# A transformer on one core: the order of the first stage's work and of the end of the sparse stages

## The reference, cut to what matters

```python
def swiglu(x, w_gate, w_up, w_down):
    return (jax.nn.silu(x @ w_gate) * (x @ w_up)) @ w_down

# first block, per layer l (stage 0 is the first line for l = 0)
y = swiglu(rms_norm(x, ffn1_pre_g[l]), ffn1_w_gate[l], ffn1_w_up[l], ffn1_w_down[l])
x = x + 0.5 * rms_norm(y, ffn1_post_g[l])
# second block, per layer l ("sparse" stage, then "relu" stage)
u_pool, q, k, v, iq, ik, iw = jnp.split(rms_norm(x, g_pre_mix[l]) @ w_in[l], ...)
mix = jnp.concatenate([pool_mixer(u_pool, ...), dsa_attention(q, k, v, iq, ik, iw, topk)], -1) @ w_out[l]
x = x + rms_norm(mix, g_post_mix[l])
f = jnp.square(jax.nn.relu(rms_norm(x, g_pre_ffn[l]) @ w_ff1[l])) @ w_ff2[l]
x = x + rms_norm(f, g_post_ffn[l])
```

## Time and profile before

| what | us |
|---|---|
| median of 3 runs | 1866.11 (1865.77 to 1866.67) |
| the profiled execution | 1865.99 |
| its span in the trace | 1864.0 |
| PE busy | 1839.5 (99%) |
| DVE busy | 1315.5 (71%) |
| ACT busy | 1042.3 (56%) |
| POOL busy | 216.2 (12%) |
| moved from memory | 336.62 MB, 181 GB/s over the span |

### The profile page before, as it was taken

One profiled execution on the slowest core, in us unless ns is written; L12 is line 12 of the kernel. 1 busy time (PEld: TensorE's weight loads), 2 busy tenths in 40 slices (PEclk: granted clock), 3 DMA queues, 4 the chain that ended last, 5 costly groups with the idle time before them and its releaser, 6 DMA issues.

```text
span 1864.0 us, 27880 instructions
## 1 busy us (share of the span) xinstructions
PE 1839.5 (99%) x10911; PEld 1610.8 (86%) x10911; DVE 1315.5 (71%) x1734; ACT 1042.3 (56%) x1503; POOL 216.2 (12%) x264
## 2 busy tenths in 40 slices
PE   6999999999999999999999999999999999999998
PEld 6888899888888888889998988888888888888887
DVE  5766758776766776676687677666886667787665
ACT  5555545655655565555466566556755545665453
POOL 1010101010100011001021000002201111301110
PEclk9999999999999999999999999999999999999999
DMA  8585663355566557766344446655546654636561
GB/s 296 182 295 189 171 199 119 114 181 170 185 201 202 181 185 234 256 170 224 124 136 139 168 138 224 202 179 168 180 136 205 196 186 165 226 100 206 181 200 71
DMA packets 229971, 339.46 MB, mean 182 GB/s; under 512 B 22278, under 2 KB 178064, under 8 KB 229840
## 3 DMA queue, kind: packets, MB, share of 16 engines
q1 hardware_dynamic: 221968, 307.91, 50.2%
q0 software_dynamic: 7872, 29.78, 4.8%
HBM read 336.62 MB, written 1.05 MB: 181 GB/s over the span
## 4 chain that ended last, share of the span: by engine, by line
PE 93%; DVE 5%; ACT 1%; DMA 1%; issue 0%; DVEq 0%; SPq 0%; ACTq 0%
PE ps L1670 90%; PE ps L1675 3%; DVE wlo L1095 2%; DMA raw<-ffn_w_gate 1%; DVE region L1103 1%; DVE mlo L1095 1%; DVE xn L1095 0%; DVE ahl L1095 0%; ACT region L690 0%; DVE xs L1103 0%; DVE region L1593 0%; DVE sm L1591 0%; DVE hlo L1095 0%; DVE small L1111 0%; ACT ahl L690 0%
## 5 line engine op out<-in xcount | busy, mean ns | idle before, releaser
L1095 DVE TENSOR_TENSOR wlo<-raw,whi 128x1024 fp32r<-128x1024 f32 (+2 forms) x458 | 560.2, 1223 | 174.1 <-ACT whi L690 138.4
L690 ACT ACTIVATE whi<-raw 128x1024 fp32r<-128x1024 f32 (+2 forms) x458 | 482.5, 1054 | 66.2 <-PE ps L1670 16.0
L1670 PE MATMUL ps<-ahl,whi 128*128 128x512 f32 (+1 forms) x1920 | 433.5, 353 | 0.3
L1670 PEld LDWEIGHTS ps<-ahl,whi 128*128 128x128 f32 x1920 | 331.4, 190 | 43.0 <-DVE hlo L1095 0.9
L690 ACT ACTIVATE region<-ps 128x512 f32<-128x512 f32 (+2 forms) x260 | 150.1, 577 | 336.0 <-PE ps L1670 251.7
L1670 PE MATMUL ps<-whi,ahl 128*128 128x512 f32 (+2 forms) x1120 | 303.1, 348 | 8.7 <-DVE ahl L1095 7.7
L1670 PE MATMUL ps<-ahl,wlo 128*128 128x256 f32 x1568 | 269.3, 283 | 0.0
L1670 PEld LDWEIGHTS ps<-ahl,wlo 128*128 128x128 f32 x1568 | 233.4, 191 | 11.9
L1670 PEld LDWEIGHTS ps<-whi,ahl 128*128 128x128 f32 x1120 | 197.4, 190 | 35.0 <-DVE ahl L1095 10.0
L1095 DVE TENSOR_TENSOR mlo<-raw,mhi 128x1024 fp32r<-128x1024 f32 x130 | 160.8, 1237 | 47.2 <-ACT mhi L690 37.7
L1670 PE MATMUL ps<-wlo,ahl 128*128 128x512 f32 (+2 forms) x560 | 191.3, 342 | 0.0
(11 more groups left out here) (166 smaller groups left out, 2380.1 us busy)
## 6 DMA issues: line engine op xcount, KB each, us to landing
raw<-w_ff SPq DMA_DIRECT2D x64, 1024.0 KB, 5.4
raw<-ffn_w_gate SPq DMA_DIRECT2D x44, 1024.0 KB, 5.3
raw<-ffn_w_up SPq DMA_DIRECT2D x44, 1024.0 KB, 5.5
raw<-ffn_w_down SPq DMA_DIRECT2D x44, 1024.0 KB, 4.9
raw<-w_in SPq DMA_DIRECT2D x38, 1024.0 KB, 6.1
raw<-w_out SPq DMA_DIRECT2D x16, 1024.0 KB, 4.9
raw<-xa_wk SPq DMA_DIRECT2D x8, 1024.0 KB, 5.2
raw<-xa_wv SPq DMA_DIRECT2D x8, 1024.0 KB, 5.0
```

Of the source, the lines that this page charges most:

```text
L690: e.activation(o, i, f, **kw).then_inc(*act.did(*names))
L1095: e.tensor_tensor(o, a, b, op).then_inc(*dve.did(*names))
L1670: m = e.matmul(o, l, r, start=start, stop=stop)
```

## The change

It has two parts that act. The first is a function `begin` on ACT, DVE and PE in place of the `turn` of stage 0. SP loads the first gain itself, right behind the tokens m = 0; item 0 comes as two transfers of half an item with a semaphore each; POOL sends the second gain when item 0 has landed. PE turns the identity 6 times ahead of the first tokens and 12 times behind them, into a bank that nobody reads, and may start with the first four of eight row blocks when the first half of item 0 is split (`lo_half`). The product's order is now item 0 for both tiles, then item 1 for both. DVE weighs the first half of tokens m = 1 before the second half of item 0 is split; ACT sums the squares of tile 0 before it takes the tokens (1, 0). The second part is in the sparse stages: DVE's `head(2)` stands behind `out(0)` and `out(1)`, and the item of `take(s, "w_out2", 2)` is split earlier, on DVE in two pieces around `out(2)` and `turned(3)`, on ACT ahead of `turned(3)`. In `turn` the branches for stage 0 go away; other stages keep their order.

```diff
             x_half(0)
+            e.dma_start(GV[:, 0:DM], gains[0][1][0][1].partition_broadcast(128)).then_inc(*gain0_in.did(("gain", 0)))
             e.dma_start(CS[:, 0:128], A["c_small"][:, 0:128]).then_inc(*const_in["ident"].did(("in",)))
-            load(0)
+            dst, src = raw_of(0).rearrange("p (k n) -> p k n", k=8), items[0][1]
+            e.dma_start(dst[:, 0:4, :], src[:, 0:4, :]).then_inc(*half_in.did(("raw", 0)))
+            e.dma_start(dst[:, 4:8, :], src[:, 4:8, :]).then_inc(*raw_in[0].did(("raw", 0)))
             x_half(1)
             load(1)
...
-            gain_load(0)
+            q.wait_ge(*raw_in[0].at("raw", 0))
             gain_load(1)
...
@@ in scalar @@
+            def begin():
+                i0, i1 = first_items(0)
+                split_to(i0, halves=1)
+                halves(0, 0, 0, 0)
+                split_to(i0)
+                halves(0, 0, 1, 1)
+                row_square(0, 0)
+                halves(0, 1, 0, 2)
+                split_to(i1, halves=1)
+                halves(0, 1, 1, 3)
+                split_to(i1)
+                row_square(0, 1)
+                split_to(i1 + 1)
+                scales(0)
@@ in scalar, sparse @@
                 exps("s", l, 3, 256, sP, 1.0)
+                take(s, "w_out2", 2)
                 turned(3)
                 post_square(s + 1, 0)
-                take(s, "w_out2", 2)
                 halves(s + 0.5, 1, 1, TILEBANK[1])
                 take(s, "w_out2", 3)
...
@@ in vector @@
+            def begin():
+                i0, i1 = first_items(0)
+                for h in range(2):
+                    q.wait_ge(*x_in[0].at("x", 0))
+                    weighted(0, 0, h)
+                split_to(i0, halves=1)
+                halves(0, 0, 0, 0)
+                q.wait_ge(*x_in[1].at("x", 1))
+                weighted(0, 1, 0)
+                split_to(i0)
+                halves(0, 0, 1, 1)
+                halves(0, 1, 0, 2)
+                weighted(0, 1, 1)
+                split_to(i1, halves=1)
+                halves(0, 1, 1, 3)
+                mean_square(0, 0)
+                split_to(i1)
+                mean_square(0, 1)
+                ts(eq, qm, TIMES[1] ** -2.0 * EPS, None, ALU.mult, ALU.bypass, ("eq", 0))
+                split_to(i1 + 1)
@@ in vector, sparse @@
                 select(1)
-                head(2)
                 out(0)
                 out(1)
+                head(2)
...
                 turned(2)
+                split_to(number[s, "w_out2", 2] + AHEAD, halves=1)
                 out(2)
                 turned(3)
+                take(s, "w_out2", 2)
                 weigh(s + 1, 0)
                 out(3)
                 renew(s + 1, 0, (0,))
                 halves(s + 0.5, 1, 1, TILEBANK[1])
                 renew(s + 1, 0, (1,))
-                take(s, "w_out2", 2)
                 take(s, "w_out2", 3)
...
@@ in tensor @@
+            def begin():
+                def awake(n):
+                    for _ in range(n):
+                        turned(PS[:, 6, 0:128], IDN, 128)
+                it = first_items(0)
+                awake(6)
+                turn_tokens(0, 0, 0)
+                turn_tokens(0, 0, 1)
+                awake(12)
+                for i, n in enumerate(it):
+                    hi, lo = halves_of(n)
+                    for m in range(2):
+                        ms = slice(m * 128, (m + 1) * 128)
+                        for k in range(8):
+                            if (i, m, k) == (0, 0, 4):
+                                turn_tokens(0, 1, 0)
+                            if (i, m, k) == (0, 1, 0):
+                                turn_tokens(0, 1, 1)
+                            if (i, m, k) == (1, 1, 7):
+                                turn_scales(0)
+                            q.wait_ge(*dve.at("lo_half" if k < 4 else "lo", n))
+                            q.wait_ge(*dve.at("a", 0, m, k // 4))
+                            ...
+                            three(PS[:, m, i * 256:(i + 1) * 256], ahv[:, k, ms], alv[:, k, ms], hi[:, k, :], lo[:, k, :], k == 0, k == 7, *names)
```

More of the change, by code:

```diff
@@ L300, in build @@
         w1_in = Done(sem("w1_in"), 16)
+        half_in, gain0_in = [Done(sem(n), 16) for n in ("half_in", "gain0_in")]
         stored = Done(sem("stored"), 16)
-        every = [pe, act, dve, pool, *raw_in, *gain_in, *x_in, *const_in.values(), region_in, mem_in, w1_in, stored]
+        every = [pe, act, dve, pool, *raw_in, *gain_in, *x_in, *const_in.values(), region_in, mem_in, w1_in, half_in, gain0_in, stored]
         IDN = CS[:, 0:128]
@@ L1125, in split_to @@
                     q.wait_ge(*act.at("hi", n, h))
-                    tt(lo[:, c], raw[:, c], hi[:, c].bitcast(F32), ALU.subtract, *([("lo", n)] if h else []))
+                    tt(lo[:, c], raw[:, c], hi[:, c].bitcast(F32), ALU.subtract, ("lo", n) if h else ("lo_half", n))
             def take(s, tag, c, ahead=AHEAD):
@@ L1132, in gain_here @@
                 i = gain_no[s, which]
-                q.wait_ge(*gain_in[i % NG].at("gain", i))
+                q.wait_ge(*(gain_in[i % NG] if i else gain0_in).at("gain", i))
                 return gain_of(s, which)
@@ L1655, in sparse @@
                 renew(s + 1, 0, (1,))
-                take(s, "w_out2", 2)
                 take(s, "w_out2", 3)
+            begin()
             for s in range(12):
-                turn(s)
+                if s:
+                    turn(s)
                 {"ffn": ffn, "relu": ffn, "hybrid": hybrid, "memory": memory, "sparse": sparse}[kind_of(s)](s)
@@ L1699, in turn_tokens, with turn_scales @@
                     blocks(s, m, half, 2 * m + half)
+            def turn_scales(s):
+                for m in range(2):
+                    q.wait_ge(*pool.at("r2", s, m))
+                    turned(PS[:, 7, m * 128:(m + 1) * 128], r2[:, m:m + 1].broadcast_to([128, 128]), 128, *([("r2_turned", s)] if m else []))
+            def begin():
[9 more added lines that the diff above has]
+                    hi, lo = halves_of(n)
+                    for m in range(2):
+                        ms = slice(m * 128, (m + 1) * 128)
[8 more added lines that the diff above has]
+                            q.wait_ge(*dve.at("a", 0, m, k // 4))
+                            names = [("used", n)] if (m, k) == (1, 7) else []
+                            names += [("first", 0, m)] if (i, k) == (1, 7) else []
+                            three(PS[:, m, i * 256:(i + 1) * 256], ahv[:, k, ms], alv[:, k, ms], hi[:, k, :], lo[:, k, :], k == 0, k == 7, *names)
             def turn(s):
                 it, by_k = first_items(s), BY_K[kind_of(s)]
-                def scales():
-                    for m in range(2):
-                        q.wait_ge(*pool.at("r2", s, m))
-                        turned(PS[:, 7, m * 128:(m + 1) * 128], r2[:, m:m + 1].broadcast_to([128, 128]), 128, *([("r2_turned", s)] if m else []))
                 parts = [(i, n, kk) for i, n in enumerate(it) for kk in range(items[n][2])]
@@ L1738, in turn @@
                 if kind_of(s) != "sparse":
-                    ahead[1][count - 1] = scales
+                    ahead[1][count - 1] = lambda: turn_scales(s)
                 ahead[0][count * 3 // 4 if by_k else 11] = lambda: turn_tokens(s, 1, 0)
```

46 lines of the change are left out of this document (15 added, 31 removed).

## The result

The changed kernel takes 1856.91 us (median of 6 runs, 1856.78 to 1857.21); the kernel before, in the same rounds, 1866.66 (1865.77 to 1866.79). The ratio is 0.9949, 95% interval 0.9936 to 0.9962: 9.75 us, 0.5%, faster. Forecast were 1859.3 us and a range whose ends the prediction works out as 1857.6 and 1862.8.

A forecast was written before the change was run, and what follows sets the result against it. PE, busy 99% of the span, was taken as the bound, so only its idle or slow time could be won: 1865.99 - 5.0 (begin) - 1.8 (sparse ends) = 1859.2, with 0.1 to the median 1859.3 us; range 1857.6 to 1862.8.

The forecast's parts named there:

- The begin: Stretch up to the turning of stage 0's scales: would end at 26.3 instead of 31.3 us, gain 5.0 us.
- curve + 1.9 us: Begin: each load lands 1.9 us after the summed GB/s curve of before passes the bytes queued up to it.
- Rival (e): Begin: item 0's split load brings nothing, first half landing no sooner than second; costs 0 to 0.5 us, counted within forecast's 0.58.
- The lower bound: Lower end, 1857.6 us: landings at the begin with 0.6 us of lag instead of 1.9 (-1.3), and head(2) (-0.4).
- The sparse ends: Ends of both sparse stages: PE's whole wait for DVE's low half goes, 0.9 us in each, 1.8 us in all.
- the head's 0.4: Sparse stages: head(2) behind the two outputs, at most 0.2 us a stage; nothing in the forecast, -0.4 at the lower end.
- (a): Begin: turnings don't bring the fast pace, or PE falls back in pauses; 1860.5 to 1861.6 us, chance 0.19.
- the full 1.2 us: Begin: first 12 matmuls and 4 turnings run slow, pushing ACT's tokens (1,0) and all behind them by 1.2 us.
- (b): Sparse ends: DVE's half split waits for a late ACT, exchanging one wait for another; 1860.2 to 1861.1 us, chance 0.09.
- (c): By 45 us: loads 5 and 6 meet POOL's queue, giving back 2 to 3 of 5.0 us; 1861.3 to 1862.3, chance 0.10.
- (d): Begin: a crawling gain transfer on SP's queue delays all loads behind it; slower, 1870.3 us if it takes 16 us, chance 0.04.
- the 1859.2 of the sum: Whole kernel: profiled 1865.99 less 5.0 for the begin and 1.8 for the sparse ends, before 0.1 to the median.

The follow-up runs named there:

- the second trace: The changed kernel run once more, unchanged, beside the kernel before: 1856.83 us, ratio 0.9946.

## Why the prediction was off

**What held.** That only PE's idle and low-paced time can be given back, and where it lies; that the first product would start near 12.2 (11.88, and 12.32 in the second trace); that it would run at 0.12 us a matmul; that a row of work on DVE would then set the end (DVE's order of these steps, changed in one point, moves the end by 0.8 us or more); that the shift would stay until the first sparse end; that nothing comes back behind the sparse ends; that the gain on SP's queue would cost nothing.

**The begin: 5.65 us instead of 5.0.** The step that failed is the landing, "curve + 1.9 us", and with it the sentence that DVE's row starts from x1's landing. The first half came at 8.6 instead of 9.1, the second at 10.1 instead of 10.7, x1 at 11.4 instead of 12.2. The curve of bytes was taken from a trace in which two queues work; with the gain on the same queue the lag behind the bytes is smaller. The changed kernel's own line of GB/s, summed in the same way, passes the 1.64 MB of the first half at 7.6 us and the 2.69 MB of x1 at 10.3, and they land 1.0 and 1.1 us later, not 1.9. With the gain on POOL's queue again x1 landed at 12.8, 2.3 us behind the same number of bytes: the lag goes with the second queue.
The forecast had x1 land at 12.2, just when DVE would have been done with the first half's work (12.2 too), so it couldn't tell which of the two sets the end, and it chose x1. The traces say the first half: in the changed kernel DVE was busy until 11.73 with x1 there since 11.4, and with item 0 in one transfer the scales moved by 1.5 to 1.9 us though x1 came only 0.4 later. Rival (e) put that price at 0 to 0.5, for the same wrong reason. Since the first half came 0.5 us sooner, DVE's row ran some 0.4 us ahead of the forecast throughout (weighing at 11.83 instead of 12.2, tokens (1,1) done at 18.3 instead of 18.75), and PE's last stretch took 7.3 us instead of 7.5: 25.66 with the scales' turning, 26.3 forecast. The lower bound had a smaller lag, with 1.3 us for it. 0.4 us of the 5.65 are luck: the traced run of the changed kernel had the earliest rise of the pace of all, and in the second trace the gain is 5.3.

**The sparse ends: 3.1 us instead of 1.8** (3.09 between the traces of before and after, 3.17 in the experiments). Two terms were wrong. First the size of the wait. I took the 0.91 us of idle time in brackets. That counts from the modelled end of the last matmul, 1390.66. But a matmul of 512 columns is followed by the next after 0.23 us: it would have started at 1390.49 and started at 1391.57, 1.08 us late. With a second small pause in the first matmuls behind it (1392.96 to 1393.29 where 0.24 is usual) and 0.08 us of a longer first matmul, 1.23 us were to be won at each end, 2.5 in all. Take the distance between starts, not the idle time. Second, head(2), which I put at nothing, with 0.4 us as the bound: it is 0.5. The reason was not the one weighed, PE getting the outputs sooner, but DVE's pause of 0.46 us in the middle of its pooled steps. That pause stood in the timeline of before, named as DVE waiting for itself:

```profile
1365.76 1.00 DVE L1103 SCALAR_TENSOR_TENSOR ahl<-ps,sm,ahl 128x256 fp32r<-128x256 f32 x2 [0.46 <-DVE ahl L1103]
```

My range put the head's 0.4 and the smaller lag together, but held the wait's size for known: that is why the time fell below it.

**The rivals.** (a) came true in part: the pace rises during the turnings or with the first matmuls, at 9.7 to 12.4 us in kernels with this begin, and a late rise costs 0.4 us through the turnings themselves, which then run too long. It isn't the full 1.2 us, because PE doesn't start the product at the low pace. The rule of the Trainium skill (TensorE: Matmul & The Clock Gate, Part 4: PE-mode transpose), that the full clock doesn't engage for work in transpose mode, does not hold in this trace, if its transposes are these turnings (the kernel issues them with `transpose`; the trace names them MATMUL): at 9.7 us PE had done nothing but turnings, and the pace rose from 0.22 to 0.11 us a turning. And without the turnings the scales come 1.2 to 1.6 us later, so they weren't lost labour. (b), (c), (d) and (e) didn't occur: ACT's high half started 0.1 us behind its last exponent (1367.60) and the copy was taken right behind it (1369.85); the waits of PE that are left lie at 11.88 and 14.80; the gain landed at 6.6; the halves landed 1.5 us apart.
Both misses together are 1.9 us (0.65 and 1.3); 0.1 lies behind the last matmul and 0.2 is the time around the span, 1.8 us instead of the 2.0 that I carried over: that is the whole way from the 1859.2 of the sum to the profiled 1856.97.

## What to carry to other kernels

Where PE is 99% busy, ask what DVE does in the 10 us ahead of each wait: a wait of 1 us at a stage's end was two splits standing in front of a step that PE needed, while DVE had stood idle twice just before. At a kernel's begin the order on one in-order queue is the schedule: put first what the first step needs, cut what gates a chain in two, and keep another queue's bytes off until it has landed. Size a wait by the distance between the starts of two matmuls, not by the idle time that is shown, and if work is added only to raise PE's pace, count it at the low pace too: past the moment at which the real work is ready it delays it.

## What the runs showed of the hardware that was not expected

- Turnings alone raise PE's pace (0.22 to 0.11 us each), at 9.7, 10.5, 11.0 or 12.0 us in four traces of the same begin; in a fifth it rose at 12.4, with the product's first matmul. The first record of the granted clock begins at these moments; what comes before it is shown as 1.00 though PE keeps the pace of the 1.2 GHz level.
- Without them PE kept 0.21 us a matmul from 11.9 to 17.3 us, with no two starts more than 0.36 us apart in that stretch.
- A transfer of 0.5 MB took 5.4 us behind another on SP's queue and 7.5 us from POOL's queue beside it.
- Beside POOL's steps a piece of a split on DVE took 1.99 us instead of 1.23, and POOL's second step 2.13 us, where its first took 1.28 and its steps of the same shape take 1.31 on the page of before.
- DVE paused 0.46 us with its input ready, at the same step of the first sparse stage in all three traced kernels with one order of instructions, and in none with the other.
